# Two of four chunk inversions started five steps ahead of the other two, with the first scan step placed among the last steps of the trailing pair

## The reference

```python
m = jnp.where(strict, jnp.einsum('bhncd,bhnsd->bhncs', k_beta, k) * decay, 0.0)
t_inv = lax.linalg.triangular_solve(eye + m, eye, left_side=True, lower=True, unit_diagonal=True)
...
def step(state, inp):                       # lax.scan over the chunks
    v_new = u_i - einsum('bhcd,bhde->bhce', w_i, state)
    o = einsum(q_i * exp(g_i), state) + einsum(a_i, v_new)
    state = state * exp(g_last) + einsum(k_dec, v_new)
...
fwd = gated_delta_rule_chunked(q, k, v, g[:, :, 0], beta[:, :, 0])
bwd = flip(gated_delta_rule_chunked(flip(q), flip(k), flip(v), ...))
```

## Time and profile before

| what | value |
| --- | --- |
| median of three timed runs | 1057.03 us |
| profiled execution, time | 1057.9 us |
| profiled execution, span | 1056.1 us |
| PE busy | 972.5 us, 92% |
| DVE, ACT, POOL busy | 499.6, 470.4, 450.8 us |
| mean granted TensorE clock | 0.977 |

### The profile page before, as it was taken

One profiled execution on the slowest core, in us unless ns is written; L12 is line 12 of the kernel. 1 busy time (PEld: TensorE's weight loads), 2 busy tenths in 40 slices (PEclk: granted clock), 3 DMA queues, 4 the chain that ended last, 5 costly groups with the idle time before them and its releaser, 6 DMA issues.

```text
span 1056.1 us, 12807 instructions
## 1 busy us (share of the span) xinstructions
PE 972.5 (92%) x5186; PEld 820.8 (78%) x5186; DVE 499.6 (47%) x812; ACT 470.4 (45%) x821; POOL 450.8 (43%) x253
## 2 busy tenths in 40 slices
PE   6999798759999899999998979899999999999987
PEld 5987576649999797777776758788888888888876
DVE  5057764487675345324246432433333333564434
ACT  6464566435654144334376541453333433332223
POOL 4528344570002363143577642245354443454440
PEclk9999999869999899999999999999999999999998
DMA  9423110000001007133322222133323232333302
GB/s 352 133 77 98 62 41 1 1 1 1 2 27 55 1 22 259 52 120 100 89 72 61 64 86 71 47 114 100 100 83 117 80 107 93 100 100 100 100 20 80
DMA packets 25162, 84.07 MB, mean 80 GB/s; under 512 B 2992, under 2 KB 3248, under 8 KB 24976
## 3 DMA queue, kind: packets, MB, share of 16 engines
q1 hardware_dynamic: 24240, 82.14, 23.9%
q10 hardware_dynamic: 864, 1.12, 0.3%
HBM read 79.06 MB, written 2.10 MB: 77 GB/s over the span
## 4 chain that ended last, share of the span: by engine, by line
PE 74%; DVE 12%; ACT 8%; POOL 3%; issue 2%; DMA 0%; SPq 0%; DVEq 0%; ACTq 0%
PE bank L1889 72%; DVE qk L1439 2%; PE bank L1897 2%; ACT wh L1111 1%; ACT L1111 1%; POOL wl L1005 1%; DVE xl L1433 1%; DVE dd L1433 1%; DVE vc L1439 1%; ACT sl L1111 1%; DVE mp L1433 1%; ACT ee L1111 1%; ACT xs L1111 1%; ACT qk L1111 1%; DVE xf L1433 1%
## 5 line engine op out<-in xcount | busy, mean ns | idle before, releaser
L1005 POOL TENSOR_TENSOR wl<-raw,wh 128x1024 fp32r<-128x1024 f32 (+1 forms) x131 | 316.6, 2421 | 389.8 <-ACT wh L1111 389.7
L1889 PE MATMUL bank<-xh,wh 128*128 128x512 f32 (+1 forms) x536 | 207.8, 388 | 6.8 <-DVE xl L1433 4.8
L1889 PE MATMUL bank<-xh,wl 128*128 128x512 f32 (+1 forms) x536 | 205.9, 384 | 0.0
L1889 PE MATMUL bank<-xl,wh 128*128 128x512 f32 (+1 forms) x536 | 205.9, 384 | 0.0
L1111 ACT ACTIVATE wh<-raw 128x1024 fp32r<-128x1024 f32 (+1 forms) x131 | 135.7, 1042 | 133.5 <-PE bank L1889 127.3
L1889 PE MATMUL bank<-wh,xh 128*128 128x512 f32 (+1 forms) x352 | 140.1, 398 | 18.1 <-POOL wl L1005 10.4
L1889 PE MATMUL bank<-wh,xl 128*128 128x512 f32 (+1 forms) x352 | 135.0, 384 | 0.0
L1889 PE MATMUL bank<-wl,xh 128*128 128x512 f32 (+1 forms) x352 | 134.8, 383 | 0.0
L1889 PEld LDWEIGHTS bank<-xh,wh 128*128 128x128 f32 x536 | 101.5, 189 | 28.2 <-issue 6.0
L1889 PEld LDWEIGHTS bank<-xh,wl 128*128 128x128 f32 x536 | 101.4, 189 | 19.8
L1889 PEld LDWEIGHTS bank<-xl,wh 128*128 128x128 f32 x536 | 101.5, 189 | 19.0
(11 more groups left out here) (249 smaller groups left out, 1566.4 us busy)
## 6 DMA issues: line engine op xcount, KB each, us to landing
raw<-in_wflat SPq DMA_DIRECT2D x127, 512.0 KB, 3.4
xt<-in_xt SPq DMA_DIRECT2D x8, 256.0 KB, 4.3
h<-in_x SPq DMA_DIRECT2D x4, 512.0 KB, 6.8
h<-in_x SPq DMA_DIRECT2D x1, 2048.0 KB, 9.7
gain<-in_pr SPq DMA_DIRECT2D x3, 512.0 KB, 3.4
consts<-in_cf SPq DMA_DIRECT2D x1, 1472.0 KB, 10.8
raw<-in_wflat SPq DMA_DIRECT2D x4, 272.0 KB, 10.9
kh<-kh SPq DMA_DIRECT2D x8, 128.0 KB, 2.3
```

The lines of the kernel that those rows point to most:

```text
L1005: e.tensor_tensor(WL[u % NS][:, 0:n], RAW[u % NS][:, 0:n], WH[u % NS][:, 0:n].bitcast(F32), ALU.subtract).then_inc(w_lo.up(u), 1)
L1889: return e.matmul(o, l, r_, start=start, stop=stop, skip_group_check=part)
```

## The change

Before, every chunk had its two decay steps first and the rounds of all four began behind them. Now chunk 0 gets three more steps and chunk 3 gets five before the rounds begin, so that both have their first five steps behind them, and chunks 1 and 2 begin with their first step inside the rounds. One attention step stands behind each of the seven entries of that prelude. The rounds are fourteen: in each one, chunks 0 and 3 have two attention steps behind each step, chunks 1 and 2 have one. Then `z_gain` and, in five rounds for chunks 1 and 2 alone, the steps of r = 0 of the scan for both directions. POOL's `scan_keys` of r = 0 waits for the inverses of chunks 0 and 3 in place of 0 and 2. The dd products (DVE) and the mr copies (ACT) leave `inv_m` and become a step of their own, `inv_dd`. No arithmetic is added or taken away.

```diff
@@ -515,6 +515,7 @@
         do("inv_m", cb)
         yield
+        do("inv_dd", cb)
         for d in range(2):
             take(("mt", d), (inv_v, ("dt", cb, 0, d)))
         do("inv_mt", cb)
@@ -600,51 +627,30 @@
-    step(gi[1], 2)
     BI.over((0, 1, 2, 3, 4))
     gs = swa()
...
-    for g in gi[2:]:
-        step(g, 2)
-    live = True
-    while live:
-        live = False
-        for g in gi:
-            live = step(g) or live
-            step(gs, 2)
-    do("z_gain")
+    for cb, n in ((0, 1), (3, 2), (0, 1), (3, 1), (0, 1), (3, 1), (3, 1)):
+        step(gi[(0, 3, 1, 2).index(cb)], n)
+        step(gs)
+    for _ in range(14):
+        for g in gi:
+            step(g)
+            step(gs, 2 if g in gi[:2] else 1)
     while step(gs):
         pass
+    do("z_gain")
     emptied[5], emptied[6], emptied[7] = (swa_a, ("p", 31)), (swa_a, ("pt", 31)), (swa_v, ("o", 3))
     BI.over(range(8))
     G = BI
...
+    ga, gb = scan_step(0, 0), scan_step(1, 0)
+    for n in range(5):
+        for g in gi[2:]:
+            step(g)
+        if 0 < n < 3:
+            step(ga)
+            step(gb)
@@ -669,7 +675,8 @@
-        ga, gb = scan_step(0, r), scan_step(1, r)
+        if r:
+            ga, gb = scan_step(0, r), scan_step(1, r)
@@ -1060,7 +1067,7 @@
             if r == 0:
                 on.wait_ge(*inv_v.at(("t", 0, 1)))
-                on.wait_ge(*inv_v.at(("t", 2, 1)))
+                on.wait_ge(*inv_v.at(("t", 3, 1)))
                 on.wait_ge(*swa_g.at(3))
@@ -1256,7 +1263,7 @@
-        def inv_m(cb):
+        def inv_mr(cb):
             for d in range(2):
                 on.wait_ge(*inv_g.at(("m", cb, d)))
                 act(WORK[cb]["MR"][d][:], MP[cb][:, d, :], ACT.Copy, inv_a.up(("mr", cb, d)))
@@ -1601,6 +1608,9 @@
                 tt(MP[cb][:, d, :], psum[b][:, :], W["MB"][d][:], ALU.mult, inv_v.up(("m0", cb, d)))
+
+        def inv_dd(cb):
+            W = WORK[cb]
             for d in range(2):
                 on.wait_ge(*inv_g.at(("m", cb, d)))
                 tt(h3(W["DD"][d][:]), h3(MP[cb][:, d, :]), bc4(cf("LM", 7 * (1 - d))), ALU.mult, inv_v.up(("dd", cb, 0, d)))
```

More of the change, by code:

```diff
@@ L553, in swa, with scan_keys, scan_step @@
                 yield
+    def scan_keys(d, r):
+        if r:
+            BI.take(("nw", d, r), (scan_a, ("nw", d, r)))
+        do("scan_keys", d, r)
+    def scan_step(d, r):
+        if r == 0:
+            scan_keys(d, 0)
+        BI.take(("vn", d, r), (scan_a, ("vn", d, r)))
+        do("scan_v", d, r)
+        yield
+        if r:
+            BI.take(("qs", d, r), (scan_v, ("o", d, r)))
+        if r < 3:
+            BI.take(("s", d, r), (scan_v, ("s", d, r)))
+        BI.take(("av", d, r), (scan_a, ("o0", d, r)) if o_first(d, r) else (scan_v, ("o0", d, r)))
+        do("scan_o", d, r)
+        yield
+        if r < 3:
+            scan_keys(d, r + 1)
+        yield
+    o_first = lambda d, r: r < 2
+    chunk = lambda d, r: r if d == 0 else 3 - r
+    o_last = lambda cb: ("o", 1, 3 - cb) if cb < 2 else ("o", 0, cb)
     g2, g3 = gates(), swa_prep()
@@ L1420, in scalar_engine @@
         return dict(begin=begin, x_split=x_split, rms_row=rms_row, prep=prep, stat=stat, split=split, conv=conv, square=square, qsum=qsum, qexp=qexp, to_tok=to_tok,
-                    gate1=gate1, gate2=gate2, rope_root=rope_root, rope_t=rope_t, tok=tok, inv_decay=inv_decay, inv_m=inv_m,
+                    gate1=gate1, gate2=gate2, rope_root=rope_root, rope_t=rope_t, tok=tok, inv_decay=inv_decay, inv_dd=inv_mr,
                     inv_d=inv_d, swa_s=swa_s, swa_t=swa_t, swa_o=swa_o, scan_keys=scan_keys, scan_v=scan_vn, scan_o=scan_o,
@@ L1876, in vector_engine @@
         return dict(begin=begin, x_split=x_split, conv_rms=conv_rms, scale=scale, split=split, masks=masks, conv=conv, qexp=qexp, gate1=gate1, gate2=gate2, rope_sq=rope_sq,
-                    rope_root=rope_root, rope_scale=rope_scale, rope=rope, rope_t=rope_t, inv_decay=inv_decay, inv_kq=inv_kq, inv_m=inv_m,
+                    rope_root=rope_root, rope_scale=rope_scale, rope=rope, rope_t=rope_t, inv_decay=inv_decay, inv_kq=inv_kq, inv_m=inv_m, inv_dd=inv_dd,
                     inv_mt=inv_mt, inv_x=inv_x, inv_d=inv_d, inv_x7=inv_x7, inv_t=inv_t, swa_s=swa_s, swa_t=swa_t, swa_o=swa_o,
```

## The result

| | before | after |
| --- | --- | --- |
| median of 4 runs each, us | 1057.14 | 1103.34 |
| their spread, us | 1056.55 to 1059.70 | 1102.68 to 1104.15 |
| ratio, 95% interval | | 1.0424, 1.0403 to 1.0445 |
| span of the profiled execution, us | 1056.1 | 1101.5 |
| PE busy in it, us | 972.5 | 1029.4 |

The account below looks back on a forecast made before the run. PE time lost to idling and half clock was taken as the bound, 35.6 us before. After: start 13.5, rounds 8.7, attention's end 1.5, scan 7.7, sum 31.4; 4.2 less gives 1052.8 us, 8-in-10 range 1046.5 to 1058.5.

Parts of the forecast that it names:

- the full rounds: Rounds behind the one with both dd: PE idles 1.3 us for all the rest, as before.
- the idling at the start (1.5): Half clock after PE has hardly anything to do, about 195.8 to 199: costs 1.5 us, bounds 0 and 2.9.
- at the scan (2.5): Half clock for the D products behind the scan's idling: costs 2.5 us, lower bound 0.
- the round with both dd: DVE has 11.4 us against PE's 6.6; PE waits 3.5 us for dt of chunk 2, bounds 1 and 8.
- D: Rival, slower: 16 D products each wait 0.6 us for ACT's dt copy, 9.6 us, 1062.4 us; chance 0.08.
- the recovery at 202.6: Trace before: clock fell to 0.50 after idling ending at 197.87; products ran at half speed to about 202.6.
- The start: From 188 us to X's end near 208.5: 10.8 us lost as walked, 13.5 with port, clock and gap terms.
- The port: At the start, dd pairs beside POOL's masks of at take 3.42 us against 2.34, twice on the path: 2.2 us.
- The rounds' waits: From 208.5 on, PE waits 2.1 + 1.8 + 3.5 + 1.3 = 8.7 us for DVE, ACT and the ring of five banks.
- The end of the attention: Last score's maximum stands behind four xf halves on DVE: PE idles 1.5 us, between 0.5 and 2.
- The scan: PE waits 3.6 and 1.1 us for POOL's vb, 0.55 for DVE: idle 5.25, with clock 7.7 us.
- The sum: Lost PE time 31.4 us against 35.6 before, 4.2 less: 1052.8 us against the median of 1057.03.

Follow-up runs that it names:

- e1: The changed kernel with 24 extra plain f32 products, results unused, behind D of level 3 of chunk 3: 1060.0 us, ratio 1.0008.
- e2: The changed kernel with 48 extra rounded products behind D of level 3 of chunk 3: 1112.51 us, ratio 1.0506.
- f3: The changed kernel with dd and the turn of mp in steps of their own, no product added: 1053.04 us, ratio 0.9954.
- f1: The changed kernel with 53 plain f32 filler products ahead of PE's waits: four of five runs 1048.7 to 1053.0 us, ratio 0.9925; the fifth 1104.93.
- h1: The kernel before with DVE's mask of X of level 3 of chunk 0 repeated four times: 1106.09 us, ratio 1.0453.
- g1: f3 with 48 plain f32 filler products at the start, at three transposes of pm and at the scan: 1053.32 us, ratio 0.9965.
- g2: g1 without the fillers at attention transposes 10, 12 and 13: 1052.03 us, ratio 0.9949.

## Why the prediction was wrong

**The step that failed** is "so I take the 1.3 us of before for the rest", said of the full rounds. With it the clock of the rounds was left at the 1.00 of before. The prediction itself priced the half clock twice, behind the idling at the start (1.5) and at the scan (2.5), and between them it forecast itself a wait of 3.5 for PE in the round with both dd, without asking what the clock does behind that wait. It fell, and in rounded products it stayed for 112.6 us: 56.3 us of work at double time. No rival held this; D, the slower one, had another mechanism (a wait of 0.6 for each of 16 D); PE waited for ACT's dt once, 1.24 at 234.22. The windows of before could not show it: in its rounds PE is held up for 1.3 us in 106 and the clock never falls, and the recovery at 202.6 that the prediction cites came in plain f32 products of k and q.

The Trainium skill (TensorE: Matmul & The Clock Gate, section "Part 1: The HAM clock gate") says that the clock returns to full after a sustained busy stretch. The products of k and q, the burst of e1 and the rounded products of 256 columns at 725 agree. The changed kernel and e2 don't: a PE that is busy 111.86 of 113 us, or 10.50 of 10.50, stayed at 0.50. The measurement decides.

**The start** went as walked, apart from the clock. POOL and DVE in the changed kernel:

```profile
197.22 2.48 POOL L1049 TENSOR_TENSOR mp<-mp,consts 128x512 f32<-128x512 f32 x2
199.68 3.38 POOL L1043 TENSOR_TENSOR at<-at,consts 128x512 f32<-128x512 f32 x2
```

```profile
198.52 3.42 DVE L1440 TENSOR_TENSOR dd<-mp,consts 128x512 fp32r<-128x512 f32 x2 [1.74 <-POOL mp L1049]
```

The identity of chunk 0 ends at 199.7 (199.5 forecast), and the dense stretch begins at 209 with 20.91 of 21. PE idled 9.0 us from 188 to 209 (10.8 and 2.2 forecast, less 1). The second X of level 1 starts at 210.75 and takes 1.95, so it ends some 2 us late. The half clock went on until 216.9: from 209 on these are 7.9 us without a hole, half of them lost, 3.9 and with what lies before 209 more, where 1.5 was taken and 2.9 was the upper bound.

**The port.** Both dd pairs of the start took 3.42, as forecast (the second at 205.11), and a third one beside the masks 3.43, which the prediction did not count. The prediction read the 2.34 of the earlier trace rows as a pair without a block. That was wrong. In DVE's rows above, the pair at 250.28, with POOL idle, took 1.28. A dd alone takes 0.68 and beside a POOL operation 1.74; 2.34 is one of each. So the 4.7 that the prediction took for the two pairs of one round was met by 3.43 + 1.28, by luck. POOL's at goes from 1.28 to 1.72 in the same pairs. This is the Trainium skill's rule on the shared port pair (SBUF — State Buffer, "SBUF: two separate sides"), and the slowed pair lies directly ahead of the dt for which PE waits at 249.82.

**The rounds' waits.** Forecast were 2.1, 1.8, 3.5 and 1.3, 8.7 in all. From 230 to 363 PE was idle 2.84 + 1.42 + 1.14 = 5.4. The round with both dd has 1.42 + 1.14 = 2.56 of it, forecast 3.5. Part of the rest is hidden by PE's own half clock, so it is no clean test of the sizes.

**The end of the attention**: one wait of 1.54, forecast 1.5.

```profile
379.77 0.41 PE L1907 MATMUL bank<-consts,pm 128*128 128x128 f32 x2 [1.54 <-ACT pm L1118]
```

**The scan.** POOL's chain is as walked; the waits of 3.6 and 1.1 for vb did not come:

```profile
382.60 1.26 POOL L1063 TENSOR_TENSOR mix<-mix,swo 128x512 f32<-128x512 f32 x1 [31.00 <-DVE swo L1440]
383.83 4.96 POOL L1056 TENSOR_TENSOR mix<-mix,rparams 128x512 f32<-128x512 f32 x4
388.74 1.04 POOL L1081 TENSOR_TENSOR vb<-vt,beta 128x512 f32<-128x512 f32 x1
```

vb is ready 8.3 us behind the first D at 381.50 (9.0 forecast), but D and X took twice their time at half clock and ended at 391.8. At full clock, in f3, PE did wait for vb, 0.99 and 0.84. The second nw waited 0.53, forecast 0.55.

**The sum.** With the clock kept up the change is worth 0.5 to 0.7%: ratio 0.9954 in f3 and 0.9925 in f1, where 1052.8 / 1057.03 = 0.9960 was forecast. That these come so close to the forecast is in part luck, for they are other kernels, and the forecast's terms did not come one by one: of idling PE it had 12.0 + 8.7 + 1.5 + 5.3 = 27.5 us, and the changed kernel has 9.0 + 5.4 + 1.5 + 0.5 = 16.4, some of it hidden by the half clock. The order of the waits was foreseen, and the answer was wrong by 50 us since one coupling, from a wait to the clock of all that follows, was left out.

**Open.** Which of the waits between 233 and 250 brings the clock down in the changed kernel was not told apart; h1 only shows that 1.35 us can be enough. What in a plain f32 product raises the clock (that it is recorded as two instructions, its values) wasn't tried, nor why rounded products of 256 columns do it and those of 128 do not. Nor is it known why f1 fell in one run of five, or why f3 and g1 have runs at 1059.5. Of the versions that beat both kernels, f1 has the best median and risks 54 us; f3 and g2 are the ones to keep.

## What to carry to other kernels

Before a change that adds a wait to a dense stretch, ask of the trace at which clock that stretch runs, what its instructions are, and where the next kind of work stands in which the clock was seen to rise. If the clock falls, the price of the wait is not its own length: all the work up to there takes twice its time. Read PE's busy share only beside the granted clock: 100% busy at 0.50 was the worst stage of this kernel. If a hole can't be closed, place the kind of work that has been seen to bring the clock back (here plain f32 products, or rounded ones of 256 columns) right behind it.

## What the runs showed of the hardware

- A stretch of mostly rounded 128x128 products stayed at half clock for 112.6 us with PE busy 99%, and 48 of them without a gap (10.44 us) did not raise the clock; 24 plain f32 products (6.79 us) did, and after a wait of 3.41 us fourteen rounded ones of 256 columns did too (from 725.87 on).
- A single hole of 1.35 us, with one of 0.17 ahead of it, took the clock to 0.50 for 105.8 us (h1); the kernel before has a mean of 1.00 in the same stage.
- A DVE product of two SBUF tiles takes 0.68 us alone and 1.74 beside POOL's; POOL's own goes from 1.28 to 1.72.
